# Grouped-head scores from stacked high and low parts, taps moved into the opening, and token-major roots of the latent keys, in a two-block transformer kernel

## The chip, the cores and the metric

One NeuronCore of a Trainium2 chip runs the whole program. The metric is the device time of one execution in microseconds (us). The engines are named as in the profile: PE is TensorE (matrix products), PEld its weight loads, DVE is VectorE, ACT is ScalarE, POOL is GpSimd, SP is SyncE, whose queue starts the DMAs.

## What is computed

Two transformer blocks of depth 2 on 256 tokens of width 1024, all in float32. The change touches only the second block's projection and attention, which are these lines of the reference:

```python
def project_tokens(h, p, rope_m, rope_g):
    z = h @ p['w_in']
    ...
    q_m = rms_norm_2(q_m, p['g_mla_q'])
    k_m = rms_norm_2(k_m, p['g_mla_k'])
    if rope_m is not None:
        ...
    q_g = rms_norm_2(z_gq.reshape(b, n, GQA_HEADS, GQA_HEAD_DIM), p['g_gqa_q'])
    k_g = rms_norm_2(z_gk.reshape(b, n, GQA_KV_HEADS, GQA_HEAD_DIM), p['g_gqa_k'])
    if rope_g is not None:
        cos, sin = rope_g
        q_g = apply_axial_rope(q_g, cos, sin)
        k_g = apply_axial_rope(k_g, cos, sin)

def attention_block(q, k, v, scale):
    s = jnp.einsum('bqhgd,bkhd->bhgqk', q, k).astype(jnp.float32) * scale
    p = jax.nn.softmax(s, axis=-1)
    return jnp.einsum('bhgqk,bkhd->bqhgd', p.astype(v.dtype), v)

def conformer_conv(z_glu, p):
    a, g = jnp.split(z_glu, 2, axis=-1)
    y = depthwise_conv(a * jax.nn.sigmoid(g), p['conv_dw_w'], p['conv_dw_b'])
```

There are 8 latent heads (`q_m`, `k_m`) of 96 channels, the last 32 of them with rope, 8 grouped query heads (`q_g`) of 64 on 2 key heads (`k_g`), and a convolution of 31 taps over 512 channels. Layer 0 runs this for 256 context tokens (no rope) and for the 256 tokens of x (with rope, which attend to 512 keys), layer 1 for the context's keys and values alone and for x.

## The kernel before

The program is written out by hand, engine by engine: each engine has its own list of instructions, and semaphores join them. The first block and its feed-forwards come first; the second block is a row of four **streams** (`STREAMS`): stream 0 is the context in layer 0, stream 1 is x in layer 0 (rope), stream 2 is the context in layer 1 and makes only keys and values ("not full"), stream 3 is x in layer 1 (rope). Channels lie on the partitions and the 256 tokens in the free dimension.

A weight matrix is cut into blocks of 128x128, sixteen to a tile, in the order in which PE takes them. A **half** is eight blocks. ACT copies a half into its rounded high part (`high_halves`, L1846), DVE subtracts that from the whole to get the low part (`lows`, L2603), and PE multiplies block by block with three products: high by high, high by low, low by high (`three`, L822). There is room for three halves, so ACT can start half u only when PE has finished half u-3. A **pair** (`split_one`, `split_pairs`) is 16 blocks, two halves, into one PSUM bank. The `among` argument puts a small product behind each block of a pair.

A full stream opens with the projections (halves 0 to 19), then come the queries' rank product, the query heads `q_m`, the keys `k_m`, and then the pairs of the merge gates from half 20 on. In **stream**'s part "gates": pair 0 (halves 20, 21) has the sums of squares of the latent queries among it (L1502: one column per head and token tile), pair 1 (halves 22, 23) follows, then **`latent_key_sums`** (L1423): four products of 96x96 ones by 512 columns, whose result is the sum of squares over the 96 channels of each latent key, repeated on 96 partitions. ACT takes the square root of 96x2048 (L2239), and DVE the reciprocal of 96x256 head by head (L3156, eight of them, with `lows` between), then scales the keys (`scale_keys`, L3107, 96x2048). In rope streams PE multiplies queries and keys by the rotation (L1515, L1521, L1527) between pairs, DVE combines them with sine and cosine and ends with a memset that signals `roped`.

DVE also computes the depthwise convolution as 31 taps over four channel blocks (L3127, 128x256 each). Before the key reciprocals it runs taps 0 to 22 of blocks 0 to 2; `for tap in range(19, 23)` has `lows(t, tap + 4)` before each tap, so the low part of half 24 comes after tap 20.

For stream 2 the key sums are issued inside stream 3: behind its opening product (`split_opening`, halves 0 and 1) and ahead of its next pairs. There ACT has made the highs of halves 0 to 3 before it waits for the sums (`high_halves(STREAMS[3], 4)`), and DVE's eight reciprocals have `lows(STREAMS[i + 1], 5 + j)` between them.

The attention is a loop over 16 heads, 8 latent (keys of 96) and 8 grouped (64). In iteration j PE transposes the probabilities of head j (`turn`, L1569), computes the scores of head j+2 (L1552, two products of 512 columns in a rope stream), and weighs the values of an earlier head (L1586). The scores are float32 products. DVE takes each row's maximum (`row_max`, L3216), ACT the exponentials (L2311) and the copy of the transposed probabilities (L2323). DVE fills its remaining time with taps: in a rope stream the last eight of blocks 0 to 2 in the iterations of the latent heads, and block 3's spread over iterations 0 to 12.

## Time and profile before

| | us |
|---|---|
| median of 3 runs | 2583.94 |
| lowest, highest | 2579.0, 2584.39 |
| the profiled execution | 2575.13 |
| its span (first to last instruction) | 2573.3 |
| PE busy in it | 2537.3 (99%) |
| DVE busy | 2064.2 (80%) |
| ACT busy | 1292.7 (50%) |

The span is cut into stages by time: the second block's streams begin at about 1150 us. Stream 0 has its gates from about 1195 us and its attention from 1265 us; stream 1 its gates from 1650 us and its attention from 1725 us; stream 3 opens at 2080 us, with its gates from 2165 us and its attention from 2245 us. Matmul records overlap: the time of one is taken from start to start.

### The profile page before, as it was taken

To read this page: it belongs to the slowest core of one execution; us is meant where nothing else is said; L and a number is where in the kernel's file an instruction comes from. 1 tells how busy PE (TensorE), PEld (TensorE's weight loads), DVE (VectorE), ACT (ScalarE), POOL (GpSimd) and SP (SyncE) were. 2 spreads that over 40 slices of the span, in tenths; PEclk is the share of its full clock that TensorE was granted. 3 is DMA by queue.
4 is the path that set the end of the run, shared out by engine and by line. 5 is a ranking of instruction groups with operands and counts; after the bars stand their busy time and mean duration, and the time that the engine had idled before them with its cause. 6 is when DMAs were issued, how large, how long until landed. Compare 5 with 4: busy or idle time off the path is not lost.

```text
span 2573.3 us, 49828 instructions
## 1 busy us (share of the span) xinstructions
PE 2537.3 (99%) x20114; PEld 2360.8 (92%) x20114; DVE 2064.2 (80%) x3076; ACT 1292.7 (50%) x1778; POOL 52.5 (2%) x68
## 2 busy tenths in 40 slices
PE   8999999999999999999999999999999999999999
PEld 8998799999988899998889999885999988859999
DVE  7996589899876499957887876787887877978877
ACT  5345553353353453355665445546544465465543
POOL 0000000000011000000000000000000000000000
PEclk9999999999999999999999999999999999999999
DMA  7764267667632077753424554340355543404554
GB/s 293 286 237 168 95 236 287 230 269 277 220 115 99 18 272 261 261 181 144 151 99 165 181 190 184 134 162 15 134 198 190 184 149 146 164 1 148 196 181 145
DMA packets 61518, 454.60 MB, mean 177 GB/s; under 512 B 6872, under 2 KB 6896, under 8 KB 9280
## 3 DMA queue, kind: packets, MB, share of 16 engines
q1 hardware_dynamic: 54720, 394.24, 42.5%
q0 software_dynamic: 6656, 58.35, 5.8%
q8 instruction: 104, 1.70, 0.3%
q14 instruction: 38, 0.31, 0.0%
HBM read 451.49 MB, written 1.07 MB: 176 GB/s over the span
## 4 chain that ended last, share of the span: by engine, by line
PE 85%; DVE 10%; ACT 4%; issue 1%; DMA 0%; DVEq 0%; SPq 0%; ACTq 0%
PE ps L822 20%; PE ps L655 15%; PE ps L656 15%; PE ps L657 15%; PE ps L1116 3%; PE ps L1552 2%; DVE w_parts L2398 1%; PE ps L1411 1%; DVE half_parts L2603 1%; PE ps L1569 1%; PE ps L597 1%; PE ps L1586 1%; ACT half_parts L1846 1%; PE ps L1479 1%; PE ps L1423 1%
## 5 line engine op out<-in xcount | busy, mean ns | idle before, releaser
L1759 ACT ACTIVATE w_parts<-ring 128x1024 fp32r<-128x1024 f32 x462 | 463.1, 1052 | 347.7 <-PE ps L655 345.1
L655 PE MATMUL ps<-normed_parts,w_parts 128*128 128x256 f32 x2160 | 602.4, 279 | 1.7 <-DVE w_parts L2398 1.7
L656 PE MATMUL ps<-normed_parts,w_parts 128*128 128x256 f32 x2160 | 603.9, 280 | 0.0
L657 PE MATMUL ps<-normed_parts,w_parts 128*128 128x256 f32 x2160 | 603.3, 279 | 0.0
L2398 DVE SCALAR_TENSOR_TENSOR w_parts<-ring,w_parts 128x1024 fp32r<-128x1024 f32 x462 | 544.5, 1219 | 18.4 <-ACT w_parts L1759 17.4
L822 PE MATMUL ps<-stream_high,half_parts 128*128 128x256 f32 x2288 | 437.5, 287 | 3.2 <-DVE half_parts L2603 2.3
L655 PEld LDWEIGHTS ps<-normed_parts,w_parts 128*128 128x128 f32 x2160 | 406.0, 188 | 2.3 <-DVE w_parts L2398 2.3
L657 PEld LDWEIGHTS ps<-normed_parts,w_parts 128*128 128x128 f32 x2160 | 406.0, 188 | 0.0
L656 PEld LDWEIGHTS ps<-normed_parts,w_parts 128*128 128x128 f32 x2160 | 405.8, 188 | 0.0
L2603 DVE SCALAR_TENSOR_TENSOR half_parts<-ring,half_parts 128x1024 fp32r<-128x1024 f32 x233 | 281.5, 1214 | 117.5 <-ACT half_parts L1846 116.8
L822 PEld LDWEIGHTS ps<-stream_high,half_parts 128*128 128x128 f32 x2288 | 358.2, 188 | 9.5 <-issue 7.9
L655 PE MATMUL ps<-act_parts,w_parts 128*128 128x256 f32 x1232 | 344.1, 279 | 1.0 <-DVE w_parts L2398 1.0
L656 PE MATMUL ps<-act_parts,w_parts 128*128 128x256 f32 x1232 | 344.5, 280 | 0.0
L657 PE MATMUL ps<-act_parts,w_parts 128*128 128x256 f32 x1232 | 344.1, 279 | 0.0
L1846 ACT ACTIVATE half_parts<-ring 128x1024 fp32r<-128x1024 f32 x233 | 243.8, 1058 | 191.5 <-PE ps L822 162.4
L822 PE MATMUL ps<-stream_low,half_parts 128*128 128x256 f32 x1144 | 319.2, 279 | 0.0
L655 PEld LDWEIGHTS ps<-act_parts,w_parts 128*128 128x128 f32 x1232 | 231.6, 188 | 2.2 <-issue 1.4
L2485 DVE CUSTOM_DVE_ANT_0 arena<-arena 128x1024 f32<-128x1024 f32 x192 | 227.2, 1221 | 7.6 <-DVE vec L2565 6.5
L657 PEld LDWEIGHTS ps<-act_parts,w_parts 128*128 128x128 f32 x1232 | 231.6, 188 | 0.0
L656 PEld LDWEIGHTS ps<-act_parts,w_parts 128*128 128x128 f32 x1232 | 231.5, 188 | 0.0
L822 PEld LDWEIGHTS ps<-stream_low,half_parts 128*128 128x128 f32 x1144 | 215.4, 188 | 4.3 <-issue 4.1
L3127 DVE SCALAR_TENSOR_TENSOR arena<-arena,vec 128x256 f32<-128x256 f32 x360 | 154.0, 481 | 2.4
(504 smaller groups left out, 3826.5 us busy)
## 6 DMA issues: line engine op xcount, KB each, us to landing
ring<-in_weights SPq DMA_DIRECT2D x373, 1024.0 KB, 4.8
arena<-in_mod_weights POOLq DMA_DIRECT2D x32, 1536.0 KB, 6.7
arena<-in_cond POOLq DMA_DIRECT2D x8, 512.0 KB, 6.0
arena<-toeplitz_rows POOLq DMA_DIRECT2D x1, 1536.0 KB, 10.5
x<-in_x SPq DMA_DIRECT2D x1, 1024.0 KB, 4.8
arena<-in_ctx POOLq DMA_DIRECT2D x1, 1024.0 KB, 9.5
out<-x SPq DMA_DIRECT2D x4, 256.0 KB, 2.6
arena<-in_rope POOLq DMA_DIRECT2D x1, 640.0 KB, 11.7
```

The source lines that it names most:

```text
L655: first = pe.matmul(into, wh, high, start=start, stop=False, skip_group_check=True)
L656: pe.matmul(into, wh, low, start=False, stop=False, skip_group_check=True)
L657: return first, pe.matmul(into, wl, high, start=False, stop=stop, skip_group_check=True)
L822: mm = pe.matmul(into, stationary, moving, start=start and n == 0, stop=stop and n == 2, skip_group_check=True)
L1116: mm = pe.matmul(ps[:, mm_n[0] % 4, m * S:(m + 1) * S], w.take(), mixed[i][:, k, :], start=(k == 0), stop=(k == KT - 1))
L1552: mm = pe.matmul(ps[:, two_banks(j) + tt, 0:keys], q[:, tt * P:(tt + 1) * P], k, start=True, stop=True)
L1759: a(w_parts[:, to, 0, cols], ring[:, at, cols], ACT.Copy).then_inc(s["w_high"], 1)
L1846: a(half_parts[:, u % 3, 0, :], ring[:, tile % RING, half * HALF:(half + 1) * HALF], ACT.Copy).then_inc(s["half_high"], 1)
L2398: return stt(out=out, in0=whole, scalar=1.0, in1=high, op0=ALU.mult, op1=ALU.subtract)
L2485: ins = nc.vector.tensor_tensor_reduce(into, mod_w[half][:, q, :], cond_row[c], 1.0, 0.0, ALU.mult, ALU.add, mod_part[:, at, c:c + 1])
L2603: stt(out=half_parts[:, u % 3, 1, :], in0=ring[:, (t["tile"] + tile) % RING, half * HALF:(half + 1) * HALF], scalar=1.0, in1=half_parts[:, ...
L3127: ins = stt(out=conv[:, b, :], in0=src, scalar=wt, in1=conv[:, b, :], op0=ALU.mult, op1=ALU.add)
```

## The change

1. **Key sums as columns.** `latent_key_sums(at)` is now one product of one column, with the squares as weights, for each of 8 heads and 2 token tiles. The sixteen stand behind the sixteen blocks of a pair: of pair 2 (halves 24, 25) in full streams, of the first pair behind the opening product (halves 2, 3) in stream 3 for stream 2. The sums lie token by token on 128 partitions and 16 columns.
2. **Roots and rows.** ACT's root is of 128x16, DVE's reciprocal of 128x16. DVE then writes them out 96 times (a copy of 128x1536, `root_table`) and PE turns that by 16 transposes (`latent_key_rows`, L1439 after) into PSUM, one pair later; DVE scales the keys from there. The eight reciprocals of 96x256 are gone.
3. **Order around it.** In rope streams the pairs and the rotations are shifted by a pair or so, with the same number of pairs in all; the first rotation waits for `mk_normed`. DVE runs taps 23 to 26 of blocks 0 to 2 between the steps of the rope.
4. **Grouped heads.** In rope streams the grouped scores come from rounded parts: for each head and token tile one product with the high query stacked twice over high and low key (128 rows) and one of the low query with the high key (64 rows), each of 512 columns. ACT makes the copies in iterations 0, 2 and 3 of the attention, DVE the low parts in iteration 4 (`grouped_lows`).
5. **Taps in the attention.** Blocks 0 to 2 have taps 27 to 30 left, in iterations 0 to 3; block 3's run by the table `taps_by`, in rope streams up to iteration 14.

The core of the diff:

```diff
+            def latent_key_sums(at):
+                j, tt = at // NT, at % NT
+                mm = pe.matmul(ps[:, 4, at:at + 1], sq[0:QK, j, tt * P:(tt + 1) * P], C("ones", 1)[0:QK], start=True, stop=True)
...
+            def latent_key_rows(t):
+                pe.wait_ge(s["key_rows"], 2 * t["i"] + 1)
+                for j in range(MH):
+                    for tt in range(NT):
+                        to = (j % 2) * S + tt * P
+                        mm = pe.transpose(ps[0:QK, 4 + j // 2, to:to + P], root_table[:, tt, j, :], C("ident"))
+                mm.then_inc(s["key_rows"], 1)
...
                 if full:
+                    split_one((0, 1), among=latent_key_sums if i == 3 else None)
                     split_one((0, 1))
-                    split_one((0, 1))
+                    if i == 3:
+                        latent_key_rows(STREAMS[2])
                     split_pairs(2)
...
-                latent_key_sums(t)
-                gates_at()
+                pe.wait_ge(s["mk_sq"], i + 1)
+                split_one((0, 1), among=latent_key_sums)
+                split_pairs(1)
+                latent_key_rows(t)
                 if t["rope"]:
+                    split_pairs(1)
+                    pe.wait_ge(s["mk_normed"], i + 1)
...
+                            pe.matmul(into, grouped_q[half][:, b, tokens], grouped_k[half][:, 0:keys], start=True, stop=False)
+                            mm = pe.matmul(into, grouped_q_low[half_rows[half], b, tokens], grouped_k[half][half_rows[half], 0:keys], start=False, stop=True)
...
+                    high_halves(t, 28)
                 actv.wait_ge(s["mk_ss"], i + 1)
-                root(std_flat, sums, QK).then_inc(s["mk_std"], 1)
+                root(key_roots, ps[:, 4, 0:MH * NT], QK).then_inc(s["mk_std"], 1)
...
+                    if t["rope"] and j == 0:
+                        for half, r in enumerate(half_rows):
+                            a(grouped_k[half][r, 0:keys], k_g[r, 0:keys], ACT.Copy)
+                    if t["rope"] and j in (2, 3):
+                        for r in half_rows:
+                            ins = a(grouped_q[j - 2][r, :, :], q_g[half_rows[j - 2], :, :], ACT.Copy)
...
-                if not full:
-                    lows(STREAMS[i + 1], 4)
+                lows(*((t, 28) if full else (STREAMS[i + 1], 4)))
                 dve.wait_ge(s["mk_std"], i + 1)
+                link(nc.vector.reciprocal(key_roots, key_roots))
+                nc.vector.tensor_copy(root_table, roots).then_inc(s["key_rows"], 1)
+                lows(*((t, 30) if full else (STREAMS[i + 1], 6)))
+                dve.wait_ge(s["key_rows"], 2 * i + 2)
+                scale(kf, V("g_mla_k", l)[0:QK], ps[0:QK, 4:8, :].rearrange("p b (m t) -> p (b m) t", m=2)).then_inc(s["mk_normed"], 1)
...
+                def grouped_lows():
+                    dve.wait_ge(s["part_high"], 9 * n)
+                    for half, r in enumerate(half_rows):
+                        stt(out=grouped_k[half][half_rows[1 - half], 0:keys], in0=k_g[r, 0:keys], scalar=1.0, in1=grouped_k[half][r, 0:keys],
+                            op0=ALU.mult, op1=ALU.subtract)
+                        ins = stt(out=grouped_q_low[r, :, :], in0=q_g[r, :, :], scalar=1.0, in1=grouped_q[half][r, :, :], op0=ALU.mult, op1=ALU.subtract)
+                taps_by = (4, 5, 6, 7, 7, 7, 10, 13, 14, 17, 18, 21, 24, 27, 28, 31) if t["rope"] else (4, 6, 8, 10, 10, 12, 14, 16, 18, 20, 22, 25, 28, 31, 31, 31)
...
+                    if j < HEADS - 1:
+                        depthwise_conv((3,), range(taps_by[j], taps_by[j + 1]))
```

PE, stream 0, where pair 1 ends and pair 2 begins (half_parts are the split weights, half_low is the semaphore of their low parts). Before:

```order
L822 MATMUL ps<-stream_low,half_parts 128x256
L822 MATMUL ps<-stream_high,half_parts 128x256
L1423 MATMUL ps<-arena,const 96x512 [waits mk_sq,q_summed]
L1423 MATMUL ps<-arena,const 96x512 x3
L822 MATMUL ps<-stream_high,half_parts 128x256 [waits half_low,mm_evac]
L822 MATMUL ps<-stream_low,half_parts 128x256
L822 MATMUL ps<-stream_high,half_parts 128x256 x2
```

and after:

```order
L828 MATMUL ps<-stream_low,half_parts 128x256
L828 MATMUL ps<-stream_high,half_parts 128x256
L828 MATMUL ps<-stream_high,half_parts 128x256 [waits mm_evac,half_low,mk_sq,q_summed]
L828 MATMUL ps<-stream_low,half_parts 128x256
L828 MATMUL ps<-stream_high,half_parts 128x256
L1429 MATMUL ps<-const,arena 128x1
L828 MATMUL ps<-stream_high,half_parts 128x256
```

The sums, four products ahead of pair 2, now stand one behind each of its blocks (the first of sixteen is shown), and the first product behind pair 1 is one that waits for a half's low part.

DVE, stream 3's opening, from the lows of halves 2 and 3 on. Before:

```order
L2603 SCALAR_TENSOR_TENSOR half_parts<-ring,half_parts 128x1024 [waits half_high] x2
L3156 RECIPROCAL arena<-arena 96x256 [waits mk_std]
L2603 SCALAR_TENSOR_TENSOR half_parts<-ring,half_parts 128x1024 [waits half_high]
L3156 RECIPROCAL arena<-arena 96x256
L2603 SCALAR_TENSOR_TENSOR half_parts<-ring,half_parts 128x1024 [waits half_high]
L3156 RECIPROCAL arena<-arena 96x256
...
L3156 RECIPROCAL arena<-arena 96x256
L2603 SCALAR_TENSOR_TENSOR half_parts<-ring,half_parts 128x1024 [waits half_high]
L3107 SCALAR_TENSOR_TENSOR arena<-arena,vec 96x8x256 [waits dve_step]
L2603 SCALAR_TENSOR_TENSOR half_parts<-ring,half_parts 128x1024 [waits half_high] x8
```

and after:

```order
L2637 SCALAR_TENSOR_TENSOR half_parts<-ring,half_parts 128x1024 [waits half_high] x2
L3186 RECIPROCAL arena<-arena 128x16 [waits mk_std]
L3188 COPY arena<-arena 128x1536 [waits dve_step]
L2637 SCALAR_TENSOR_TENSOR half_parts<-ring,half_parts 128x1024 [waits half_high] x2
L3141 SCALAR_TENSOR_TENSOR arena<-arena,vec,ps 96x8x256 [waits key_rows]
L2637 SCALAR_TENSOR_TENSOR half_parts<-ring,half_parts 128x1024 [waits half_high] x14
```

The semaphore mk_std says that ACT's root is done. The low parts of halves 4 and 5 now stand together behind the copy, and half 6 and those behind it stand behind the scaling, which waits for PE's transposes (key_rows).

PE, stream 1's attention, iteration 6 of the loop (the turn of head 6 and the scores of head 8, the first grouped one). Before:

```order
L1569 MATMUL ps<-const,arena 128x128 [waits at_e]
L1569 MATMUL ps<-const,arena 128x128 x7
L1552 MATMUL ps<-arena 128x512 [waits at_pt]
L1552 MATMUL ps<-arena 128x512
L1586 MATMUL ps<-arena 64x256 [waits mm_evac,at_pt]
L1586 MATMUL ps<-arena 64x256 x3
```

and after:

```order
L1595 MATMUL ps<-const,arena 128x128 [waits at_e]
L1595 MATMUL ps<-const,arena 128x128 x7
L1577 MATMUL ps<-grouped_k_even,grouped_q_even 128x512 [waits part_low,at_pt]
L1578 MATMUL ps<-grouped_k_even,grouped_q_low 128x512
L1577 MATMUL ps<-grouped_k_even,grouped_q_even 128x512
L1578 MATMUL ps<-grouped_k_even,grouped_q_low 128x512
L1612 MATMUL ps<-arena 64x256 [waits mm_evac,at_pt]
L1612 MATMUL ps<-arena 64x256 x3
```

Two products have become four, and the first of them waits for the low parts as well.

## Rows read from the trace of the kernel before

**Rows 1.** The page: busy time of the engines; the chain that ended last, by engine.

```profile
PE 2537.3 (99%) x20114; PEld 2360.8 (92%) x20114; DVE 2064.2 (80%) x3076; ACT 1292.7 (50%) x1778; POOL 52.5 (2%) x68
...
PE 85%; DVE 10%; ACT 4%; issue 1%; DMA 0%; DVEq 0%; SPq 0%; ACTq 0%
```

**Rows 2.** Stream 1's gates, then attention: us, PE, PEld, DVE, ACT, POOL busy; clock; DMA.

```profile
1640.00:1720.00 80.00, 80.00 (x575) 70.32 (x574) 76.34 (x96) 42.74 (x56) 0.00 (x0) 1.00 0.43 156
1720.00:1830.00 110.00, 109.52 (x716) 79.80 (x716) 88.64 (x138) 72.23 (x118) 0.00 (x0) 1.00 0.20 75
```

**Rows 3.** PE's waits in the streams (1150 to 2573 us): total, times, longest.

```profile
PE ps L1552 <- ACT arena L2304: 1.4, 3, 0.9
PE ps L822 <- DVE half_parts L2603: 1.2, 1, 1.2
```

**Rows 4.** PE in order of time, stream 0: query sums in pair 0, key sums, pair 2.

```profile
1199.97 0.28 PE L1502 MATMUL ps<-const,arena 96*128 96x1 f32 x2
...
1200.55 0.28 PE L1502 MATMUL ps<-const,arena 96*128 96x1 f32 x2
...
1209.89 3.60 PE L1423 MATMUL ps<-arena,const 96*96 96x512 f32 x8
...
1213.44 0.28 PE L822 MATMUL ps<-stream_low,half_parts 128*128 128x256 f32 x1
...
1213.79 0.28 PE L822 MATMUL ps<-stream_low,half_parts 128*128 128x256 f32 x1
```

**Rows 5.** DVE in order of time, stream 0: low part of half 24, tap 21.

```profile
1210.48 1.22 DVE L2603 SCALAR_TENSOR_TENSOR half_parts<-ring,half_parts 128x1024 fp32r<-128x1024 f32 x1
1211.62 1.27 DVE L3127 SCALAR_TENSOR_TENSOR arena<-arena,vec 128x256 f32<-128x256 f32 x3
```

**Rows 6.** PE in order of time, stream 3's opening: key sums of stream 2.

```profile
2087.32 3.60 PE L1423 MATMUL ps<-arena,const 96*96 96x512 f32 x8
```

**Rows 7.** ACT there: root, first evacuation, highs of halves 4 and 5.

```profile
2091.02 1.88 ACT L2239 ACTIVATE arena<-ps 96x2048 f32<-96x2048 f32 x1 [3.80 <-PE ps L1423]
2092.80 0.58 ACT L2201 ACTIVATE arena<-ps 128x512 f32<-128x512 f32 x1
...
2093.74 2.01 ACT L1846 ACTIVATE half_parts<-ring 128x1024 fp32r<-128x1024 f32 x2
```

**Rows 8.** DVE there, in order of time: low part of half 4.

```profile
2094.84 1.23 DVE L2603 SCALAR_TENSOR_TENSOR half_parts<-ring,half_parts 128x1024 fp32r<-128x1024 f32 x1 [0.16 <-ACT half_parts L1846]
```

**Rows 9.** Groups by line, DVE, 1150 to 2573 us: busy, mean ns | idle before.

```profile
L3156 DVE RECIPROCAL arena<-arena 96x256 f32<-96x256 f32 x32 | 55.4, 1732 | 4.2 <-ACT arena L2239 4.2
...
L3107 DVE SCALAR_TENSOR_TENSOR arena<-arena,vec 96x2048 f32<-96x2048 f32 x4 | 9.3, 2336 | 0.0
...
L3231 DVE COPY arena<-arena 128x1024 f32<-128x1024 f32 x6 | 4.2, 694 | 0.2
```

**Rows 10.** PE in order of time, stream 1, iteration 9: scores of head 11, weighing, turn.

```profile
1768.48 1.98 PE L1552 MATMUL ps<-arena 64*128 64x512 f32 x4
1770.39 1.08 PE L1586 MATMUL ps<-arena 128*64 128x256 f32 x8
1771.41 1.09 PE L1569 MATMUL ps<-const,arena 128*128 128x128 f32 x8
1772.43 1.98 PE L1552 MATMUL ps<-arena 64*128 64x512 f32 x4
```

**Rows 11.** DVE there: a row maximum, values of the latent heads, four taps, the next maximum.

```profile
1770.86 1.22 DVE L3216 TENSOR_REDUCE arena<-ps 128x2 f32<-128x1024 f32 x1
...
1772.19 1.22 DVE L3237 TENSOR_TENSOR arena<-ps,arena 128x1024 f32<-128x1024 f32 x1
1773.34 2.04 DVE L3127 SCALAR_TENSOR_TENSOR arena<-arena,vec 128x256 f32<-128x256 f32 x4
1775.29 1.22 DVE L3216 TENSOR_REDUCE arena<-ps 128x2 f32<-128x1024 f32 x1
```

**Rows 12.** ACT, stream 1, iterations 2 and 3: copy of head 3, first exponential of head 5.

```profile
1745.33 1.05 ACT L2323 ACTIVATE arena<-ps 128x1024 f32<-128x1024 f32 x1
1747.48 0.78 ACT L2311 ACTIVATE arena<-ps,arena 128x512 f32<-128x512 f32 x1 [1.10 <-DVE arena L3217]
```

**Rows 13.** PE there: turns of heads 4 and 5.

```profile
1746.93 1.09 PE L1569 MATMUL ps<-const,arena 128*128 128x128 f32 x8
...
1750.69 1.09 PE L1569 MATMUL ps<-const,arena 128*128 128x128 f32 x8
```

More of the change, by code:

```diff
@@ L1415, in one @@
                 mm_n[0] += 1
[L1418 to L1425 removed]
+            left = {0: (s["x_ready"], 6 * QUARTERS), 1: (s["c_ready"], 2 * QUARTERS), 2: (s["x_ready"], 8 * QUARTERS), 3: (s["mk_normed"], 3)}
+            def latent_key_sums(at):
+                j, tt = at // NT, at % NT
+                mm = pe.matmul(ps[:, 4, at:at + 1], sq[0:QK, j, tt * P:(tt + 1) * P], C("ones", 1)[0:QK], start=True, stop=True)
+                if at == NT * MH - 1:
+                    mm.then_inc(s["mk_ss"], 1)
+            def latent_key_rows(t):
[5 more added lines that the diff above has]
+                mm.then_inc(s["key_rows"], 1)
             def stream(t):
@@ L1545, in scores @@
                 def scores(j):
-                    q, k, _, _ = head(j)
+                    q, k, b, half = head(j)
                     if j >= 3:
@@ L1550, in scores @@
                         pe.wait_ge(s["at_norm"], 5 * n + 2)
+                    if t["rope"] and j == MH:
+                        pe.wait_ge(s["part_low"], 8 * n)
                     for tt in range(NT):
-                        mm = pe.matmul(ps[:, two_banks(j) + tt, 0:keys], q[:, tt * P:(tt + 1) * P], k, start=True, stop=True)
+                        into, tokens = ps[:, two_banks(j) + tt, 0:keys], slice(tt * P, (tt + 1) * P)
+                        if j < MH or not t["rope"]:
+                            mm = pe.matmul(into, q[:, tokens], k, start=True, stop=True)
+                        else:
+                            pe.matmul(into, grouped_q[half][:, b, tokens], grouped_k[half][:, 0:keys], start=True, stop=False)
+                            mm = pe.matmul(into, grouped_q_low[half_rows[half], b, tokens], grouped_k[half][half_rows[half], 0:keys], start=False, stop=True)
                     mm.then_inc(s["at_s"], 1)
@@ L2275, in keep_last_gates @@
                     mm_n[0] += 1
-                std_flat, sums = std_m[0:QK].rearrange("p m t -> p (m t)"), ps[0:QK, 4:8, :].rearrange("p b t -> p (b t)")
                 if full:
@@ L3178, in stream @@
                     fold = lambda v: v.rearrange("p b (m t) -> p (b m) t", m=2)
-                    key_reciprocals(range(4))
+                    depthwise_conv((0, 1, 2), range(23, 24))
+                    lows(t, 31)
+                    depthwise_conv((0, 1, 2), range(24, 25))
+                    lows(t, 32)
                     dve.wait_ge(s["rot_m_done"], 3 * l + 1)
                     tt(sq[0:QK], fold(ps[0:QK, 4:8, :]), over(sin_m, QK, MH), ALU.mult).then_inc(s["rot_used"], 1)
-                    key_reciprocals(range(4, MH))
-                    scale_keys()
+                    lows(t, 33)
+                    depthwise_conv((0, 1, 2), range(25, 26))
+                    lows(t, 34)
+                    depthwise_conv((0, 1, 2), range(26, 27))
                     lows(t, 35)
@@ L3253, in stream @@
                         low_part(1, latent_parts, weighed)
-                    if t["rope"] and j < MH:
-                        depthwise_conv((0, 1, 2), range(23 + j, 24 + j))
-                        if j != 3:
-                            depthwise_conv((3,), range(4 + j - (j > 3), 5 + j - (j > 3)))
-                    elif t["rope"] and j < HEADS - 3:
-                        depthwise_conv((3,), range(11 + 4 * (j - MH), 15 + 4 * (j - MH)))
-                    elif not t["rope"] and j != 3 and j < HEADS - 3:
-                        depthwise_conv((3,), range(4 + 2 * (j - (j > 3)) + max(0, j - 10), 6 + 2 * (j - (j > 3)) + max(0, j - 9)))
+                    if t["rope"] and j == 4:
+                        grouped_lows()
+                    if t["rope"] and j < 4:
+                        depthwise_conv((0, 1, 2), range(27 + j, 28 + j))
+                    if j < HEADS - 1:
+                        depthwise_conv((3,), range(taps_by[j], taps_by[j + 1]))
                 inverse_sums(1)
```

56 lines of the change are left out of this document (23 added, 33 removed).

## The prediction, made before the changed kernel was run

> **What bounds the kernel now.** Read the busy times first [rows 1]: PE works in 99% of the span and is 85% of the chain that ended last. Then the stages that the change touches [rows 2]: in stream 1's gates PE is busy in all 80 of 80 us and in its attention in 109.5 of 110, at the full clock, while DVE has 3.7 and 21 us to spare. Then PE's waits [rows 3]: in all the streams together none is longer than 1.2 us. So every microsecond of product that is added or taken away here moves the end, and work taken from DVE or ACT moves it only where PE waits for them. The question for each edit is what it does to PE's list, and whether PE now meets work that is not ready.
>
> **Key sums (four streams).** Four products of 512 columns go. They start at 1209.89, and the second product behind them starts at 1213.44 [rows 4], one step of 0.12 earlier the first: 3.43 us. Sixteen products of one column come, among a pair. Beside the same product of the queries a block takes 0.58 us instead of 0.35 [rows 4], so one costs 0.23 and sixteen 3.7. That is +0.3 a stream, +1.1 in all: the sums get no cheaper. Bounds: 0.14 to 0.23 for each column, -1.2 to +0.3 a stream; I take the measured step.
>
> **Transposes (four streams).** Sixteen new ones on PE. Eight turns take 1.02 us [rows 10], so 2.0 us a stream, +8.1 in all. Nothing hides them. Bounds 7.4 to 9.
>
> **DVE and ACT in the openings.** Eight reciprocals of 1.73 us [rows 9] go, some 13 us a stream; a reciprocal of 128x16, a copy of 128x1536 (0.69 x 1.5 = 1.0 us by the copy of 1024) and in rope streams twelve tap products (0.4 us each by the three in 1.2 us [rows 5], 4.8) come. The key scaling of 2.3 us stays. DVE is lighter by 7 to 12 us, and ACT by 1.6 us a root. Neither was waited for there but once (1.2 us [rows 3]), so this is worth at most that 1.2 us, -1.2.
>
> **A cover that goes (streams 0, 1, 3).** The old key sums stood between pair 1 and pair 2, and behind them PE found half 24 ready. Its low part runs on DVE from 1210.48 to 1211.6 [rows 5], behind taps which don't move. PE reaches pair 2 at 1209.89 [rows 4]. Until now the 3.43 us of sums filled that time; now PE stands until 1211.6. The same rows stand in the other full streams. 1.7 x 3 = +5.2. Bounds 0 and 5.4.
>
> **Stream 3's opening.** Two waits. PE now begins pair halves 2, 3 at 2087.3 [rows 6], with sixteen columns among them: it ends at 2087.3 + 16 x 0.58 = 2096.6. Only then are the sums there, and ACT has been waiting for them with the highs of halves 4 and 5 queued behind the root: before, the root came at 2091.0 and those highs at 2093.74 [rows 7], 0.9 behind the root's end, and half 4's low at 2094.84 to 2096.0 [rows 8], just in time. After: root 2096.8 to 2097.1, evacuation to 2098.1, high 4 to 2099.1, low 4 to 2100.4. PE waits 3.8 us. It then ends the second pair, transposes, and wants half 6; but DVE has half 6 behind the scaling, which waits for these transposes: 0.1 + 2.3 [rows 9] + 1.15 [rows 5] = 3.5 us more. Together +7.3. Bounds 0 (if either is ready for a reason that I don't see) and 8. The same two places in full streams are safe: highs up to 27 stand ahead of ACT's root, lows up to 29 ahead of the scaling, and a whole pair of 5.6 us lies between the transposes and half 30. `roped` also keeps its distance, three pairs behind the last rotation.
>
> **Grouped scores (two rope streams, 16 heads).** A head's scores take 1.91 us, from 1768.48 to 1770.39 [rows 10]: two float32 products of 512 columns. They become four rounded ones of 512. The nearest rows bound one of them: two steps of a rounded 256-column product, 2 x 0.117 = 0.235 [rows 4], and an eighth of a float32 product's step, where each counts four passes, 3.43 / 16 = 0.214. With 0.1 us for the change of shape, four take 0.96 to 1.04; I take 1.0, so -0.9 a head, -14.4. Bounds -8 (if half is lost at the changes of shape) and -16.8 (nothing lost). The Trainium skill, "TensorE: Matmul & The Clock Gate", section "Wait — 56ns, not 53.3ns?", gives 215.7 ns from start to start at 512 columns; by it the four would take 0.86 us and the term would be -16.8, an estimate. This case's 0.214 agrees, but its float32 scores of four passes take 0.24 a pass, so I stay with the rows.
>
> **Does the attention keep up?** An iteration takes 3.95 us now [rows 10], 3.05 then. DVE takes 3.28 between two maxima with four taps (4.43 less 1.15 for the values [rows 11]), and 2.8 with three, which is what the new table gives: that fits. ACT needs 2.5. But DVE's new low parts in iteration 4 take 3.5 us (two of 1.15 as the values [rows 11], two half as long), where it had 1.7 us of taps. From the maximum of head 6 to that of head 9 DVE then works 1.33 x 3 + 3.5 + 1.5 + 1.5 + 0.9 (the reciprocal of the sums and their copy of 0.69 [rows 9]) = 11.4 us, PE 3.76 (a latent head's iteration [rows 13]) + 3.05 + 3.05 = 9.9. PE waits 1.5 at the scores of head 10, and 0.3 at the end, where the last taps stand ahead of the sums: +1.8 a stream, +3.6. ACT's two copies of the queries (1.9 us for both: 1.05 each as the copy in [rows 12], less the overlap of records) stand behind the copy of head 2, and again behind that of head 3 [rows 12]; head 4's exponentials were 1.6 us ahead of its turn, head 5's 1.7 (1747.48 + 1.5 against 1750.69) [rows 12, 13], and 1.1 of the second delay falls into ACT's wait. That leaves PE 0.3 and 0.5 late, +1.6 for both streams. Bounds of the two together 0 and 10. Attention: -14.4 + 3.6 + 1.6 = -9.2.
>
> **The sum.** 1.1 + 8.1 - 1.2 + 5.2 + 7.3 - 9.2 = +11.3. The change adds to the openings 20.5 us and takes 9.2 from the attentions. Against the profiled execution's 2575.1 that is 2586.4; that execution lies 8.8 under the median of the runs, 2583.9, so I set it on the median: **2595.2**.
>
> **Rivals.**
> *The openings have no waits.* If DVE and ACT reach halves 24, 4 and 6 in time, 12.5 go and the time is 2582.7, no change. Against it: the three places come from rows and from the order, with no free engine to help.
> *The attention gains in full.* No slip on DVE and ACT and 1.05 us a head: -16.8 in place of -9.2, 2587.6, still within 0.2%. For it speaks that PE has spare work between scores and turn, 4 us where DVE and ACT need 3.2.
> *Faster.* DVE, freed of 7 to 12 us a stream, runs ahead of PE instead of behind it. It would have to reach half 24 at least 1.7 us earlier, and hold that lead through iteration 4. Then both rivals hold: 11.3 - 12.5 - 7.6 = -8.8, 2575. The relief comes after half 24, which speaks against it.
> *PE's clock falls.* PE stands 3.8 and 3.5 us in stream 3; no row shows the clock after such a gap inside the kernel, it is 1.00 in all stretches [rows 2]. If a pair after each ran at half speed, 5.6 us each, +11.2: 2606.4. The Trainium skill, "TensorE: Matmul & The Clock Gate", Part 1, has the engine throttled again when it goes idle; by that rule this rival is what happens if the gaps are long enough.
> *The change doesn't do what it says.* The rounded products of 512 columns cost as much as float32 ones: no gain in the scores, 2595.2 + 14.4 = 2609.6.
>
> **How the numbers follow.** Forecast 0.62 (its own range 2589 to 2602), no waits in the openings 0.13, full attention 0.13, both 0.05, clock 0.04, no gain 0.03. I lay the range from 2581 to 2603: it leaves out the faster rival and the two slow ones. A measurement of this kernel tells 0.2%, 5.2 us, from no change. Faster 0.06 (the faster rival and a little of the first), same 0.25 (the first two), slower 0.69.
>
> **What would show it.** In the changed profile: PE's first product of pair 2 waits some 1.7 us for half_parts, three times; two waits of 3.5 to 4 us at stream 3's opening; sixteen transposes in 2.0 us; about 1.0 us from a grouped head's scores to the weighing, and iterations of 3.0 to 3.1; a wait at the scores of head 10 of 1 to 2 us; DVE's busy time some 43 us lower (55.4 [rows 9] less 5 for the tables and 7 for the low parts). The forecast is wrong if a block of pair 2 takes 0.35 us with its column, if half 6 is ready when the transposes end, or if the iterations of the grouped heads take less than 2.9 us.

## The result, and the profile of the changed kernel

| | us | |
|---|---|---|
| kernel before, median of 6 runs | 2578.07 | 2574.33 to 2584.39 |
| changed kernel, median of 6 runs | 2611.51 | 2599.72 to 2620.05 |
| changed against before | 1.0128 | 95% interval 1.0103 to 1.0152 |
| profiled execution of the changed kernel | 2617.19 | its span 2614.9 |

The changed kernel is slower, by three times the forecast +11.3 us: 2611.5 lies outside the range of 2581 to 2603. The base was too high as well. In 63 later executions of the kernel before, 55 lie between 2571.9 and 2579.4, and 8, whose granted clock averages 0.996 and not 1.000, between 2583.0 and 2588.2; two of the three runs I had set the forecast on (2583.94 and 2584.39) lie in the range of those 8. From the 2575.1 of the profiled execution the same sum gives 2586.4.

The page of the changed kernel, with the busy times that answer to [rows 1] and the granted clock in its 40 slices:

```profile
PE 2564.8 (98%) x20274; PEld 2402.2 (92%) x20274; DVE 2027.2 (78%) x3060; ACT 1296.5 (50%) x1790; POOL 52.4 (2%) x68
...
PEclk9999999999999999998999999899999999999999
```

DVE works 37 us less (43 were forecast), and the end comes 41.6 us later. PE is busy 27.5 us more, though its scores got shorter, and two digits of the clock are 8. Windows of stream 0's gates (length, PE busy, granted clock) say what that is; the trace of the kernel before has 1.00 from its 16th us to its 2572nd, in stream 1 as in [rows 2] and here too. The last row is from stream 3's opening:

```profile
1200.00:1205.00 5.00, 5.00 (x46) 1.00 0.85 293
1210.00:1215.00 5.00, 3.73 (x21) 0.73 0.48 175
1215.00:1220.00 5.00, 5.00 (x25) 0.50 0.66 233
1220.00:1225.00 5.00, 5.00 (x24) 0.50 0.03 11
1225.00:1230.00 5.00, 5.00 (x28) 0.56 0.02 3
1230.00:1235.00 5.00, 5.00 (x46) 1.00 0.24 85
...
2120.00:2125.00 5.00, 5.00 (x32) 0.66 0.53 210
```

From 1212.3 on TensorE is granted 0.50, which is 1.2 GHz, for 2.7 + 5 + 5 + 4.4 = 17.1 us. The same stretch of 17.1 us stands at the same place of streams 1 and 3, and one of 3.4 us in stream 3's opening. Each of the three long ones ends 2 to 4 us behind the last column of the pair. PE's timeline there (start, length, the wait in brackets) shows what it did before, and what a block with its column costs at either level:

```profile
1211.27 0.36 PE L828 MATMUL ps<-stream_high,half_parts 128*128 128x256 f32 x1 [1.80 <-DVE half_parts L2637]
...
1211.70 0.28 PE L1429 MATMUL ps<-const,arena 96*128 96x1 f32 x2
1211.84 0.36 PE L828 MATMUL ps<-stream_high,half_parts 128*128 128x256 f32 x1
...
1213.32 0.42 PE L1429 MATMUL ps<-const,arena 96*128 96x1 f32 x2
...
1214.39 0.42 PE L1429 MATMUL ps<-const,arena 96*128 96x1 f32 x2
...
1234.02 1.91 PE L1439 MATMUL ps<-const,arena 128*96 128x128 f32 x16
1235.68 0.37 PE L828 MATMUL ps<-stream_high,half_parts 128*128 128x256 f32 x1
```

The forecast wait on half 24 is there (1.80; 1.7 forecast); a block with its column takes 0.57 us at 1.00 and 1.07 at 0.50; the sixteen transposes take 1.7 us from start to start. PE's waits by cause in the streams (us in all, times, longest), to be read against [rows 3]:

```profile
PE ps L828 <- DVE half_parts L2637: 13.0, 6, 3.7
...
PE ps L1595 <- ACT arena L2337: 3.8, 6, 0.8
```

The 13.0 are three of 1.8, two of 3.6 to 3.7 and one of 0.3. Here are the rows of the two long ones, in stream 3's opening, on PE and on DVE; the kernel before has no wait over 1.2 us there:

```profile
2119.45 0.36 PE L828 MATMUL ps<-stream_high,half_parts 128*128 128x256 f32 x1 [3.60 <-DVE half_parts L2637]
...
2116.45 0.96 DVE L3188 COPY arena<-arena 128x1536 f32<-128x1536 f32 x1
2118.08 2.36 DVE L2637 SCALAR_TENSOR_TENSOR half_parts<-ring,half_parts 128x1024 fp32r<-128x1024 f32 x2 [0.67 <-ACT half_parts L1872]
2128.63 2.34 DVE L3141 SCALAR_TENSOR_TENSOR arena<-arena,vec,ps 96x2048 f32<-96x2048 f32 x1 [8.20 <-PE ps L1439]
```

The second wait, behind the scaling, is 3.66. Last, a grouped head of stream 1, to be read against [rows 10]; the rows of PEld are the weight loads:

```profile
1775.91 1.09 PE L1595 MATMUL ps<-const,arena 128*128 128x128 f32 x8
1776.76 0.47 PE L1577 MATMUL ps<-grouped_k_even,grouped_q_even 128*128 128x512 f32 x1
1777.16 0.50 PE L1578 MATMUL ps<-grouped_k_even,grouped_q_low 64*128 64x512 f32 x1
1777.59 0.49 PE L1577 MATMUL ps<-grouped_k_even,grouped_q_even 128*128 128x512 f32 x1
1778.02 0.50 PE L1578 MATMUL ps<-grouped_k_even,grouped_q_low 64*128 64x512 f32 x1
1778.45 1.08 PE L1612 MATMUL ps<-arena 128*64 128x256 f32 x8
1779.46 1.09 PE L1595 MATMUL ps<-const,arena 128*128 128x128 f32 x8
...
1777.59 0.19 PEld L1577 LDWEIGHTS ps<-grouped_k_even,grouped_q_even 128*128 128x128 f32 x1 [0.24 <-issue]
```

The scores take 1.69 us (1776.76 to 1778.45) where 1.91 stood and 1.0 was forecast: 0.43 a product, and the load of 0.19 starts with its own product, at 1777.59, instead of under the one ahead of it; so do the other loads of the group but the first. An iteration is 3.55 us.

Where the 41.6 us between the two profiled executions arose, by the same instruction in both traces:

| stage | forecast | measured |
|---|---|---|
| stream 0, gates | +4.0 | +10.4 |
| feed-forward between streams 0 and 1 | 0 | -2.0 |
| stream 1, gates | +4.0 | +11.8 |
| stream 1, attention | -4.6 | -0.9 |
| stream 2 and stream 3's opening | +8.4 | +10.1 |
| stream 3, gates | +4.0 | +11.8 |
| stream 3, attention | -4.6 | -0.9 |

The rest, 1.3 us, lies ahead of and behind these. The -2.0 of the feed-forward is not the change's: the stretch from its first sums of squares to the next projections takes 195.9 us in seven of the twelve traces of this record, 197.4 in three and 197.7 in two, and the kernel before is one of the last two. Why it differs is open.

### The profile page after: what moved, and what is told of

Its sections match the earlier page's. It is cut to its first block, busy times and chain, and to the rows that moved or that the text cites. A ratio compares the mean times of both kernels' runs of the same rounds, so it can differ in the third digit from the quotient of the medians.

```text
span 2614.9 us, 50147 instructions
## 1 busy us (share of the span) xinstructions
PE 2564.8 (98%) x20274; PEld 2402.2 (92%) x20274; DVE 2027.2 (78%) x3060; ACT 1296.5 (50%) x1790; POOL 52.4 (2%) x68
## 3 DMA queue, kind: packets, MB, share of 16 engines
HBM read 451.49 MB, written 1.07 MB: 173 GB/s over the span
## 4 chain that ended last, share of the span: by engine, by line
PE 81%; DVE 12%; ACT 4%; issue 1%; DMA 0%; POOL 0%; POOLq 0%; DVEq 0%; SPq 0%; ACTq 0%
PE ps L828 20%; PE ps L661 15%; PE ps L662 15%; PE ps L663 15%; DVE arena L3161 3%; PE ps L1122 3%; DVE half_parts L2637 2%; DVE w_parts L2432 1%; PE ps L1575 1%; PE ps L603 1%; PE ps L1595 1%; PE ps L1612 1%; ACT half_parts L1872 1%; DVE arena L3246 0%; DVE h L2576 0%
## 5 line engine op out<-in xcount | busy, mean ns | idle before, releaser
L828 PE MATMUL ps<-stream_high,half_parts 128*128 128x256 f32 x2288 | 472.2, 297 | 14.1 <-DVE half_parts L2637 14.1
L828 PEld LDWEIGHTS ps<-stream_high,half_parts 128*128 128x128 f32 x2288 | 378.9, 195 | 20.0 <-issue 19.4
L828 PE MATMUL ps<-stream_low,half_parts 128*128 128x256 f32 x1144 | 327.1, 286 | 0.0
L828 PEld LDWEIGHTS ps<-stream_low,half_parts 128*128 128x128 f32 x1144 | 223.8, 196 | 3.3 <-issue 3.1
```

What stands on the lines that cost most here:

```text
L828: mm = pe.matmul(into, stationary, moving, start=start and n == 0, stop=stop and n == 2, skip_group_check=True)
```

## The experiments

Two questions stood open. What makes the clock fall: PE's wait of 1.8 us, the pair with columns behind it, or both? And why does a rounded product of 512 columns take 0.43 us? Ratios are to the kernel before, run on the same chip at the same time.

**e1: the low part of half 24 early.**

```diff
                     actv.wait_ge(s["mq_ss"], n + 1)
+                    high_halves(t, 25)
...
-                    lows(t, 24)
+                    lows(t, 25)
                     depthwise_conv((0, 1, 2), range(18, 19))
```

> The changed kernel, but in the full streams ACT makes the high part of half 24 before the squares of the keys and DVE its low part before tap 18, so that PE should not stand 1.8 us ahead of pair 2 (the pair with the sixteen one-column products). Theory 'wait': the fall of the granted clock to 0.50 behind that place (17.1 us, three times) is started by the 1.8-us wait. Then the wait is under 0.5 us, the clock stays at 1.00 in pair 2, a block with its column takes 0.58 us instead of 1.07, and the time is 3 x (1.8 + 8) = 29 us under the changed kernel's, 1.000 to 1.004 of the kernel before. Theory 'columns': the one-column products alone make the clock fall. Then only 3 x 1.8 = 5 us go, the stretches at 0.50 stay, and the ratio is about 1.010.

Measured: 2589.07 us, ratio 1.0056 (1.0031 to 1.0080). No wait ahead of pair 2, and the clock stays up in the very pairs that hold the columns (windows in streams 0, 1 and 3):

```profile
1212.00:1217.00 5.00, 5.00 (x46) 1.00 0.58 211
...
1663.00:1668.00 5.00, 5.00 (x46) 1.00 0.55 210
...
2192.00:2197.00 5.00, 5.00 (x45) 1.00 0.64 210
```

By the two ratios (1.0128 and 1.0056) 0.72%, 18.5 us, have gone by an edit that moves three copies and three subtractions; the waits themselves account for 5.4. Stream 1's gates take 79.5 us instead of 89.4: 9.9 less, of which 1.8 is the wait and 8.1 the clock. The columns alone didn't bring the fall here. Of the 29 us expected 27.1 came between the two profiled spans (2614.9 and 2587.8). The ratio came out above the 1.000 to 1.004 expected for another reason: not every execution of the changed kernel has three falls (see e3), so its median had less to lose. The 7.3 us of waits in stream 3's opening stay, with a fall of 3.4 us at each of the two. One of its six executions has 2599.7 us and a mean clock of 0.993, the others 0.998 or 0.999; that one was not traced.

**e2: the kernel before, with a wait put in.** Old key sums, no columns in pair 2.

```diff
                     for tap in range(19, 23):
-                        lows(t, tap + 4)
                         depthwise_conv((0, 1, 2), range(tap, tap + 1))
+                    ...
+                    link(stt(out=half_parts[:, u % 3, 1, :], ...))
+                    lows(t, 26)
```

> The kernel before (old key sums, no one-column products in pair 2), but DVE makes the low part of half 24 only behind tap 22, and makes it twice (the same values): it ends some 2.3 us after PE has finished the key sums, so PE waits about 2.2 us ahead of a pair without columns, in three streams. Theory 'wait': the clock falls behind it as in the changed kernel, 17 us at 0.50 three times, +6.6 for the waits and +25 for the clock, ratio 1.012. Theory 'wait and columns together': the clock stays at 1.00 or falls for a short time only (the changed kernel shows 3.4 us at 0.50 behind a wait of 3.6 us in stream 3's opening), the ratio is 1.003 to 1.005.

Measured: 2583.49 us, ratio 1.0033 (1.0019 to 1.0047). PE waits 2.0 us three times. The clock falls for 3.4 us in stream 0 behind the wait, for 3.4 in stream 3 from the wait's end on, and not at all in stream 1:

```profile
1218.99 0.36 PE L822 MATMUL ps<-stream_high,half_parts 128*128 128x256 f32 x1 [2.00 <-DVE half_parts L2603]
...
1220.00:1225.00 5.00, 5.00 (x32) 0.66 0.71 233
1225.00:1230.00 5.00, 5.00 (x45) 1.00 0.44 184
...
1673.00:1678.00 5.00, 5.00 (x45) 1.00 0.80 280
```

So a wait can start a fall, but where the pair behind it is made of full products alone the clock is back at 1.00 after 3.4 us. The long fall needs the columns behind the wait: the theory "both". The other traces bear it out. Behind the two waits of 3.6 us in stream 3's opening, where full products follow, the clock falls in seven of eight places (the changed kernel, e1, e3, e4), six times for 3.4 us and once for 6.8; where a pair with columns follows a wait of 1.8 us it falls for 17.1 us or more or not at all.

**e3: both products of a grouped head with 128 rows.**

```diff
+                        for to in half_rows:
+                            ins = stt(out=grouped_q_low[half][to, :, :], in0=q_g[r, :, :], ..., in1=grouped_q[half][r, :, :], ...)
...
-                            mm = pe.matmul(into, grouped_q_low[half_rows[half], b, tokens], grouped_k[half][half_rows[half], 0:keys], ...)
+                            mm = pe.matmul(into, grouped_q_low[half][:, b, tokens], grouped_k[half][:, 0:keys], ...)
```

> The changed kernel, but the low query is stacked twice as well, so that the second product of a grouped head's scores also has 128 rows (low query by high and low key). DVE makes two more copies in iteration 4 (2 x 1.2 us). In the changed kernel each rounded product of 512 columns takes 0.43 us from start to start, while such products of 128 rows in the first block's value projection take 0.235 (0.70 for three). Theory 'shape': the alternation of 128 and 64 rows keeps the next weights from being loaded under the running product (the load of 0.19 starts with the product). Then the four products take about 1.0 us instead of 1.7, an iteration of the grouped heads 2.9 to 3.3 us instead of 3.55 (DVE with its taps may become the later one), and the time falls by 5 to 11 us in streams 1 and 3 together. Theory 'place' (keys and queries both lie in the arena at the same remainder) or 'stationary': still 0.43, no gain, DVE's 2.4 us may show as a wait of PE of about 1 us a stream.

Measured: one execution, 2595.26 us. A later grouped head of stream 1, and two loads:

```profile
1788.31 0.48 PE L1578 MATMUL ps<-grouped_k_even,grouped_q_even 128*128 128x512 f32 x1
1788.62 0.39 PE L1579 MATMUL ps<-grouped_k_even,grouped_q_low_even 128*128 128x512 f32 x1
1788.85 0.40 PE L1578 MATMUL ps<-grouped_k_even,grouped_q_even 128*128 128x512 f32 x1
1789.09 0.40 PE L1579 MATMUL ps<-grouped_k_even,grouped_q_low_even 128*128 128x512 f32 x1
1789.41 1.08 PE L1613 MATMUL ps<-arena 128*64 128x256 f32 x8
...
1766.67 0.19 PEld L1578 LDWEIGHTS ps<-grouped_k_even,grouped_q_even 128*128 128x128 f32 x1
1766.89 0.19 PEld L1579 LDWEIGHTS ps<-grouped_k_even,grouped_q_low_even 128*128 128x128 f32 x1
```

0.23 a product between one of the four and the next, 0.3 at either end, 1.10 for the four, no load of theirs behind an issue gap, an iteration of 2.97: "shape" holds. The attention still takes 70.9 us, near the changed kernel's 71.5, since PE now stands at head 8 and behind it:

```profile
1766.36 0.47 PE L1578 MATMUL ps<-grouped_k_even,grouped_q_even 128*128 128x512 f32 x1 [1.14 <-DVE grouped_q_low_odd L3279]
...
1769.38 1.09 PE L1596 MATMUL ps<-const,arena 128*128 128x128 f32 x8 [0.84 <-ACT arena L2338]
```

That is not yet the "DVE slip" of the prediction: this run gives DVE 6.3 us of low parts in iteration 4, where the changed kernel has 3.8. This run tells something of the clock too. Its openings are the changed kernel's, with waits of 1.77, 1.78 and 1.81 us ahead of the columns, and the clock stayed at 1.00 in all three pairs. So the long fall comes in one execution and not in another, and what decides it no run shows. It fits that the changed kernel's six runs spread over 20 us, with mean granted clocks from 0.989 to 0.997 (one fall of 17.1 us lowers the mean by 0.0033).

**e4: the stacked keys at another address.**

```diff
-        grouped_k = [parts("grouped_k_even", 28160, 2 * S), parts("grouped_k_odd", 28672, 2 * S)]
+        grouped_k = [parts("grouped_k_even", 28216, 2 * S), parts("grouped_k_odd", 28728, 2 * S)]
```

> The changed kernel with the two buffers of the stacked grouped keys moved by 56 words, so that the moving keys and the stationary queries start at different remainders of their addresses, as the operands of the split products do (0.117 us for 256 columns). Nothing else differs. Theory 'place': the 512-column products take about 0.235 us instead of 0.43. Theory 'shape': they stay at 0.43 us and nothing else moves.

Measured: one execution, 2603.22 us; the four products start at 1772.09, 1772.50, 1772.92 and 1773.36, still 0.41 to 0.44 apart. "Place" is out. The clock fell in one of the three pairs with columns, for 20.5 us:

```profile
1666.00:1686.00 20.00, 20.00 (x95) 0.50 0.29 106
2206.00:2226.00 20.00, 20.00 (x174) 1.00 0.45 158
```

That prices a fall inside one execution: streams 1 and 3 make the same products behind the same wait of 1.81 us, and their gates take 91.0 us with the fall and 81.6 without it. In e3, with the waits and no fall, they take 81.6 too, so the 89.4 of the changed kernel hold 7.8 for the clock.

**e6: the kernel before, with the grouped scores alone**, ordered high, high, low, low (the lines are shown against the changed kernel's). The taps that iteration 4 had go to later iterations:

```diff
                             pe.matmul(into, grouped_q[half][:, b, tokens], grouped_k[half][:, 0:keys], start=True, stop=False)
-                            mm = pe.matmul(into, grouped_q_low[half_rows[half], b, tokens], ...)
+                    if t["rope"] and j >= MH:
+                        for tt in range(NT):
+                            mm = pe.matmul(into, grouped_q_low[half_rows[half], b, tokens], ...)
```

> The kernel before with the grouped scores alone: stacked high and low keys as in the changed kernel, but both 128-row products first and then both 64-row products (two changes of shape a head instead of four); openings, key sums and roots as before. The taps of iteration 4 go to iterations 8 to 14. Theory 'shape': a change of shape costs 0.19 us, so a head's scores take 1.3 to 1.35 us instead of 1.91 (1.70 in the changed kernel); 16 x 0.6 = 9.6 us less, minus the waits for ACT's copies (0.6 + 0.8) and for DVE's low parts in each of two streams, some 5 us: about -5 us, ratio 0.997 to 0.999, attention of a rope stream 69 to 71 us instead of 72.4. Rival 'DVE': without the taps moved into the opening DVE (54.5 of 72.4 us busy, now 58.4) is late in iterations 4 to 8 and the waits eat the gain: ratio 1.000 to 1.002.

Measured: 2575.55 us, ratio 1.0000 (0.9987 to 1.0014). PE's own work in stream 1's attention is 66.7 us instead of 71.9, but the attention takes 72.1 of 72.4: the time of the rival "DVE". DVE works 58.0 of the 72.1 us, and PE waits 5.2:

```profile
PE ps L1584 <- ACT arena L2326: 3.0, 4, 1.1
PE ps L1577 <- DVE arena L3254: 1.2, 2, 0.7
PE ps L1563 <- ACT arena L2319: 1.0, 1, 1.0
```

Most of these name ACT: 1.4 us are its copies at heads 4 and 5. The longest, 1.1 at a late turn, is DVE's at one remove, since the exponentials it waits for had waited 0.74 us for a row maximum, and DVE had been at work without a gap. That DVE's load is what ate the gain is shown by e8, where twelve of the tap products stand in the opening instead.

**e7: the changed openings without waits, float32 scores.** e1's edit, and for stream 3's opening:

```diff
                 if not full:
-                    high_halves(STREAMS[3], 4)
+                    high_halves(STREAMS[3], 6)
...
-                lows(*((t, 28) if full else (STREAMS[i + 1], 4)))
+                lows(*((t, 28) if full else (STREAMS[i + 1], 6)))
...
-                lows(*((t, 30) if full else (STREAMS[i + 1], 6)))
+                lows(*((t, 30) if full else (STREAMS[i + 1], 8)))
```

> The changed kernel with float32 scores as before (no copies, no low parts of the grouped heads), and with the waits of the openings taken away: half 24's high and low early as in e1, and in stream 3's opening the highs of halves 4 and 5 ahead of the root, their lows ahead of DVE's wait for it, the lows of halves 6 and 7 ahead of the scaling. It shows what the token-major roots cost by themselves. Theory: sixteen transposes at 1.9 us and sixteen columns for four wide products, +2.1 a stream, 8.5 in all, less the 1.2 + 0.9 us of waits that the kernel before had in its openings: +6 us, ratio 1.002 to 1.003, no stretch at a granted clock of 0.50. Rival 'something else': if the openings cost more than these terms, ratio 1.005 and above, and the stages of stream 1 (77.6 us before) show over 80 us.

Measured: 2581.4 us, ratio 1.0018 (1.0000 to 1.0035). Both long waits of stream 3's opening are gone, and so is every stretch at 0.50:

```profile
1652.70:1732.20 79.50, 79.50 (x628) 1.00 0.44 154
2090.00:2115.00 25.00, 24.71 (x213) 1.00 0.55 199
```

The gates of streams 1 and 3 take 79.5 us instead of 77.6: +1.9 a stream for transposes and columns together, 2.3 forecast. One wait of 0.8 us is left in stream 0, half a pair ahead of the columns and with full products behind it; the clock stays up there.

**e8: e7's openings with the scores in e6's order.**

> e7's openings and the grouped scores of e6 (high, high, low, low) with the changed kernel's taps. Scores of a grouped head 1.3 us, iterations of 3.1 to 3.3 us; waits at heads 4 and 5 for ACT's copies (1.4 us a stream) stay. From e7's +6: 16 x 0.6 less, plus 4 to 5 us of waits, together +0.5 us against the kernel before, ratio 0.999 to 1.001. Rival 'clock': if falls of the granted clock come back without the waits, 1.003 and more.

Measured: 2575.49 us, ratio 1.0002 (0.9987 to 1.0017). A grouped head:

```profile
1776.50 0.72 PE L1577 MATMUL ps<-grouped_k_odd,grouped_q_odd 128*128 128x512 f32 x2
1777.15 0.73 PE L1581 MATMUL ps<-grouped_k_odd,grouped_q_low 64*128 64x512 f32 x2
1777.81 1.08 PE L1615 MATMUL ps<-arena 128*64 128x256 f32 x8
```

1.31 us with two changes of shape, 1.69 with four, 1.10 with none: each costs 0.1 to 0.2. The attention takes 69.4 us in streams 1 and 3: 6 us less than before in both together, which just pays for the openings. Its iterations of 3.16 us are nearly the forecast ones, DVE has the changed kernel's low parts, and PE waits 0.70 at the scores of head 10 and not at head 8. The change comes out even once its waits and its order of products are mended: by the two ratios (1.0128 and 1.0002) 1.26%, some 32 us, were not its arithmetic.

**e9: the columns in one bunch ahead of pair 2**, with e7's openings.

```diff
-                split_one((0, 1), among=latent_key_sums)
-                split_pairs(1)
+                for at in range(NT * MH):
+                    latent_key_sums(at)
+                split_pairs(2)
```

> The changed kernel with the openings' waits taken away as in e7, and the sixteen one-column products in one bunch ahead of pair 2 instead of one behind each of its blocks (full streams). It measures the price of a one-column product by itself. If 0.23 us is its own time: 3.7 us for sixteen, nothing gained. If 0.23 comes from standing alone between products of another form: 0.12 to 0.16 each, 2.0 to 2.5 us for sixteen, 1.2 to 1.7 us a stream less. Does the clock fall in a bunch of such small products? In the changed kernel it fell where they stood among a pair behind a wait; without a wait I expect 1.00.

Measured: one execution, 2587.67 us.

```profile
1666.43 3.63 PE L1429 MATMUL ps<-const,arena 96*128 96x1 f32 x32
1669.92 0.46 PE L828 MATMUL ps<-stream_high,half_parts 128*128 128x256 f32 x1
...
1669.00:1674.00 5.00, 5.00 (x31) 0.66 0.00 0
```

Sixteen take 3.49 us, 0.22 each: that is their own price, not one of standing between others, and nothing is gained. And the clock fell for 3.4 us in stream 1 and 6.8 in stream 3, not in stream 0, though PE never stood there: a bunch of such small products can do to the clock what a wait does. My 1.00 was wrong. The Trainium skill, "TensorE: Matmul & The Clock Gate", Part 1 ("What's actually happening"), has the gate follow how busy the array has been, and lists the low level as the idle one. This run doesn't contradict the first, but the second doesn't hold by the profile's account, which calls PE busy in all 5.00 of those 5 us.

**e10 and e11: a version to beat both.** e10 is e7's openings and e3's scores of 128 rows, with DVE's low parts spread over iterations 1 to 4; e11 also spreads ACT's four copies over iterations 1 to 4.

```diff
+                    if t["rope"] and j in (1, 2):
+                        dve.wait_ge(s["at_pt"], base + 2)
+                        grouped_lows(j - 1, True, False)
+                    if t["rope"] and j == 3:
+                        dve.wait_ge(s["at_e"], base + 5)
+                        grouped_lows(0, False, True)
                     if t["rope"] and j == 4:
...
+                        grouped_lows(1, False, True)
```

> e7's openings, and the grouped scores with 128 rows in both products as in e3, but DVE's low parts spread: those of the keys in iterations 1 and 2, of the even queries in 3, of the odd ones in 4; block 3's taps move to later iterations. In e3 PE lost 1.1 us at the scores of head 8 and 0.8 behind it to the 6.3 us of low parts in iteration 4. Theory: scores 1.05 us a head, iterations of the grouped heads about 3.0 us, no wait at head 8 over 0.4; the waits at heads 4 and 5 for ACT's two copies an iteration stay (1.4 us a stream): attention 67 to 68.5 us instead of 72.4, 8 to 11 us less in both, against +6 of the openings: ratio 0.998 to 1.000. Rival 'DVE': five more microseconds of low parts than DVE can hide in the latent heads, attention about 69.5 as in e8, ratio 1.000 and above.

> e10 with ACT's four copies of the queries one in each of iterations 1 to 4 instead of two in iteration 2 and two in 3. Theory: ACT's head start of 1.6 us over PE, with some 0.4 us of slack in each latent iteration, hides most of them: PE's waits at heads 4 and 5 fall from 1.4 us a stream to 0 to 0.7, ratio 0.997 to 0.999. Rival: the delay only moves on to head 6, and the time is e10's.

Measured: e10 2576.7 us, ratio 1.0006 (0.9995 to 1.0018); e11 2577.95, ratio 1.0010 (1.0000 to 1.0020). e10's attention of stream 1 takes 69.2 us, only 0.2 less than e8's with its slower products: the wait at head 8 is gone, those at the turns of heads 4 and 5 stayed (0.64, 0.80) and so did 0.71 at the scores of head 10, but both transpositions of the shares (the reciprocals of the row sums) now wait 0.7. e11 has the rival's result: the two waits for ACT's copies turned into 1.00 at a head's scores, 0.96 at a later turn and 1.31 at the shares, and the attention takes 70.1 us. Neither beats the kernel before.

## Why the prediction was wrong

**"PE's clock falls" (rival, 0.04).** This is the failed step. I asked for the clock only behind stream 3's two long waits and never behind the three of 1.7 us, although the change puts products of one column right behind these. Each such place costs some 8 us when it falls (8.1 in stream 1 by e1, 7.8 by e3), three of them 24 of the 41.6 us of the profiled pair; over the runs e1 saves 18.5 with its waits. For stream 3 I priced 11.2; it was 3.4 us at half speed, 1.7 (6.8 to 10.2 us at half speed in e1, e3 and e4). The row I had, a clock of 1.00 in all stretches before, spoke of a program without such waits, and I let it stand as evidence against.

**"Grouped scores" (-14.4).** The mechanism held, the size did not: I allowed 0.1 us a head for the change of shape, and it is up to 0.2 a product, four times a head (0.43 against the 0.23 of e3). 1.69 came instead of 1.0 (e3 shows 1.10 where no shape changes), so PE's work fell by 3.5 us and not 14.4. The Trainium skill, "TensorEngine Tiling (Array Packing)", section "Key Properties", says it: changing the tiling mode, not just the tile, drains TensorE. The loads of 0.19 that start with their product agree with it, and e3, e8 and the changed kernel put 0, 2 and 4 changes between 128 and 64 rows (the one to the weighing counted) at 1.10, 1.31 and 1.69 us. I had weighed the Trainium skill's figure for products of one kind and not this rule. A slip of wording in that term changes nothing: 0.214 us is a quarter of a float32 product's step of 3.43 / 4, not an eighth.

**"Does the attention keep up?" (+5.2).** ACT's copies cost 0.64 and 0.80 at heads 4 and 5, where 0.3 and 0.5 were forecast: right mechanism, a little small. Of DVE's slip of 1.5 at head 10 came 0.35 with iterations of 3.55, and 0.70 with those of 3.16 in e8: too high even there. e3's 1.1 at head 8 doesn't bear it out, since that run gives DVE 2.5 us more to do. Together the attentions gave 1.7 us instead of 9.2.

**"A cover that goes" (+5.2)** and **"Stream 3's opening" (+7.3)** were right to 0.2 us: 1.80, 1.81 and 1.80; 3.60 and 3.66. e7 takes all of them away by issuing highs and lows earlier, so they were an order of issue and not a shortage of DVE.

**"Transposes" (+8.1)** and **"Key sums" (+1.1)**: together 1.9 a stream in stream 1 and 3 against 2.3 forecast (e7), the transposes 1.7 a stream against 2.0, the columns 0.22 each (e9) against 0.23. **"DVE and ACT in the openings" (-1.2)**: that wait (2120.11 in the trace before) went, and with it one of 0.9 us in stream 0 that I had not counted. DVE's relief of 37 us was worth what was forecast, almost nothing by itself. It has a use only with shorter scores: e6 against e8 is the same scores without and with it, 72.1 and 69.4 us of attention.

**The rival "openings have no waits"** forecast no change, and e8 stands at 1.0002. But e8 also has another order of products, and it comes out even by other terms than that rival's: 6 us off the attentions, where the rival had 9.2.

## What to carry to other kernels

Price a new wait on TensorE not by its length alone: look at what stands behind it, and keep small products away from there, since wait and thin work together could cost some four times the wait on top of it (8 us for 1.8 here). When products of 128 and of 64 rows mix, group them by shape, and count the changes per product. And set a forecast on a median only after asking whether the few runs shown belong to one kind.

## What the runs showed of the hardware that I had not expected

- The granted clock of TensorE fell to 0.50 (1.2 GHz) for 3.4 us, twice for 6.8, behind waits of 2.0 and 3.6 us and with 3.5 us of one-column products and no wait at all; with columns in the pair behind a wait of 1.8 us it stayed down for 17.1 us, in e4 for 20.5, and came back 2 to 4 us behind the last column. It fell in three of three such places in the changed kernel's trace, one of three in e4's, none of three in e3's, and in none of the pairs with columns and no wait straight ahead of them (fifteen in e1, e7, e8, e10 and e11). Of the 43 executions of e7, e8, e10 and e11, 35 have a mean of 1.000 and 8 have 0.996; of the kernel before these are 55 and 8 of 63.
- A one-column float32 product takes 0.22 us alone as well as among others, nearly what a rounded one of 512 columns and the same 128 weight columns takes (0.23).
- A change between 128 and 64 rows costs 0.1 to 0.2 us, about the weight load of 0.19 that is then not hidden.
- Left open: what begins the 0.996 in the 8 executions of the kernel before. e10's profiled execution has a mean of 0.996 too. Its clock is 0.50 for 20.5 us in stream 0's attention, which takes 55.7 us there and 47.6 to 47.7 in every other trace, and PE had no wait over 0.9 us ahead of it, as in the traces without this fall.
